# Expert passes of a two-layer decoder: from one expert a pass to four column groups of 32 tokens

## The reference, cut to what matters

```python
logits = tok @ router_w                       # (520, 16)
scores = softmax(logits); sel = scores + router_bias
# best of 4 groups of 4 experts, then the 2 best experts inside it
combine = one_hot(eidx) * gate                # 2 experts a token, 1040 pairs
a = einsum('md,edf->mef', tok, w1)            # w1, w3: 16 x 1024 x 256 in each layer
b = einsum('md,edf->mef', tok, w3)
g = silu(a) * b * combine[..., None]
y = einsum('mef,efd->md', g, w2)              # w2: 16 x 256 x 1024
```

## Time and profile before

| | us |
|---|---|
| three runs | 1240.48, 1243.84, 1242.88 (median 1242.88) |
| profiled execution, its own time | 1236.9 |
| span of that execution in the trace | 1235.1 |
| mean granted TensorE clock | 0.867 |

### The profile page before, as it was taken

One profiled execution on the slowest core, in us unless ns is written; L12 is line 12 of the kernel. 1 busy time (PEld: TensorE's weight loads), 2 busy tenths in 40 slices (PEclk: granted clock), 3 DMA queues, 4 the chain that ended last, 5 costly groups with the idle time before them and its releaser, 6 DMA issues. The chain is left out here.

```text
span 1235.1 us, 10486 instructions
## 1 busy us (share of the span) xinstructions
PE 999.4 (81%) x3428; PEld 586.6 (47%) x3428; DVE 496.4 (40%) x1014; ACT 195.4 (16%) x452; POOL 291.8 (24%) x372
## 2 busy tenths in 40 slices
PE   6999999999999647976299999943965599999800
PEld 5644466667766512416244444423855244444400
DVE  0044443434323488687632111109286611211147
ACT  2101112212301411002011111121111011111121
POOL 0033032302221022334111122113182112111114
PEclk8999999999999955995589999985585699999965
DMA  6323568447440292446189999528660159998241
GB/s 246 127 80 132 185 211 293 167 170 283 178 140 35 65 317 59 136 140 222 50 274 312 326 332 318 200 71 313 196 220 36 34 195 312 322 341 290 108 171 71
DMA packets 123874, 237.04 MB, mean 192 GB/s; under 512 B 13335, under 2 KB 84559, under 8 KB 123174
## 3 DMA queue, kind: packets, MB, share of 16 engines
q1 hardware_dynamic: 111830, 214.46, 50.2%
q0 software_dynamic: 12000, 22.03, 4.9%
HBM read 226.79 MB, written 67.69 MB: 238 GB/s over the span
## 5 line engine op out<-in xcount | busy, mean ns | idle before, releaser
L331 PE MATMUL banks<-expert_w_a,xT 128*128 128x512 f32 x576 | 257.4, 601 | 1.2 <-ACT glu_gate L472 1.2
L331 PEld LDWEIGHTS banks<-expert_w_a,xT 128*128 128x128 f32 x576 | 152.5, 270 | 88.1 <-issue 47.1
L1494 PE MATMUL banks<-expert_w_a,moe_rowsT 128*128 128x512 f32 x288 | 131.6, 611 | 4.2 <-DVE moe_rowsT L1607 4.2
L1494 PE MATMUL banks<-expert_w_b,moe_rowsT 128*128 128x512 f32 x256 | 112.5, 592 | 0.0
L1689 POOL DMA_INDIRECT results<-moe_results,moe_put_column x34 | 34.3, 1008 | 300.6 <-DVE moe_results L1616 283.9
L1610 DVE TENSOR_TENSOR moe_gated<-moe_silu,banks 128x256 f32<-128x256 f32 x34 | 14.3, 421 | 216.2 <-ACT moe_silu L1558 216.2
L516 DVE TENSOR_TENSOR qk_rows<-banks,b_in_chunk 128x512 f32<-128x512 f32 x24 | 16.6, 692 | 191.8 <-PE banks L331 121.0
L1494 PEld LDWEIGHTS banks<-expert_w_a,moe_rowsT 128*128 128x128 f32 x288 | 55.0, 196 | 69.0 <-issue 65.7
L1494 PEld LDWEIGHTS banks<-expert_w_b,moe_rowsT 128*128 128x128 f32 x256 | 47.4, 190 | 53.6 <-issue 53.6
L1505 PE MATMUL banks<-expert_w_a,moe_gatedT 128*128 128x512 f32 x144 | 65.0, 594 | 1.0 <-DVE moe_gatedT L1613 1.0
L598 POOL TENSOR_TENSOR rope_parts<-qk_rows,constants 128x128 f32<-128x128 f32 x24 | 18.9, 789 | 198.4 <-DVE qk_rows L516 198.4
(11 more groups left out here) (280 smaller groups left out, 1392.4 us busy)
## 6 DMA issues: line engine op xcount, KB each, us to landing
expert_w_a<-in_moe_w SPq DMA_DIRECT2D x54, 1024.0 KB, 10.6
expert_w_b<-in_moe_w SPq DMA_DIRECT2D x48, 1024.0 KB, 10.7
expert_w_a<-in_w_in SPq DMA_DIRECT2D x10, 2048.0 KB, 7.9
out_s_attn<-in_cache_attn_w SPq DMA_DIRECT2D x8, 2044.0 KB, 17.9
expert_w_a<-in_cache_attn_w SPq DMA_DIRECT2D x32, 256.0 KB
join_results<-results SPq DMA_DIRECT2D x16, 512.0 KB
q_broadcast<-sample_q SPq DMA_DIRECT2D x8, 512.0 KB
rows<-h SPq DMA_DIRECT2D x8, 512.0 KB
```

The source lines that it names most:

```text
L331: last = pe.matmul(bank(k, u % 2), tile_cols(kk, c // 3, t), W[:, (c + 1) % 2, kk], start=kk == 0, stop=kk == KT - 1)
L1494: last = pe.matmul(bank(k, 2 + b), XT[:, kk], w13(slot)[:, kk], start=kk == 0, stop=kk == KT - 1)
```

## The change

A pass still has 128 slots, but they are four groups of 32. Each group belongs to one expert and uses its own quarter of PE's columns, so one pass holds up to three experts. There are 48 groups, twelve passes. Experts 0 to 3 get three groups each; the other twelve are ranked by their number of tokens, and rank r gets `BY_SIZE[r]` groups. The order in which ranks are served is `IN_TURN`. Which expert has which rank is only known at run time: SP reads its number into a register (`k.order`) and addresses the weights by it. What doesn't fit goes to further passes as before. POOL takes the row numbers straight from the table's column instead of copying the column first. The passes are written out instead of looped.

```diff
+GROUP = 32
+PER_PASS = P // GROUP
+NFIXED = 4
+FIXED = [3] * NFIXED
+BY_SIZE = [5, 4, 4, 3, 3, 3, 3, 3, 2, 2, 2, 2]
+IN_TURN = [0, 11, 1, 10, 2, 9, 3, 8, 4, 5, 6, 7]
+CAP = FIXED + [BY_SIZE[r] for r in IN_TURN]
+START = [sum(CAP[:m]) for m in range(NE)]
+GROUPS = [m for m in range(NE) for _ in range(CAP[m])]
+NB = len(GROUPS) // PER_PASS
+LAST = [(START[m] + CAP[m] - 1) // PER_PASS for m in range(NE)]
+MAX_EXTRA = 10
+NCOL = NB + MAX_EXTRA
...
@@ Router.pe_tables
+            last = pe.matmul(bank(k, 7)[:, 256:257 + NCOL], self.SL[:, n], self.valr[:, n],
...
@@ Router.dve, between the ranks and the slot table
-        for j in range(2):
-            L(tt(self.tmp[:], self.oh[:, j], rk, ALU.mult))
-            L(dve.tensor_reduce(self.rank[:, 0, j], self.tmp[:], AX, ALU.add))
...
+        L(stt(out=self.key[:], in0=counts[:, NFIXED:NE], scalar=16.0, in1=cst(k, "tie"), op0=ALU.mult, op1=ALU.add))
+        L(tt(self.larger[:], across(self.key[:], SIZES), b3(self.key[:], SIZES), ALU.is_gt))
+        L(dve.tensor_reduce(self.place[:], self.larger[:], AX, ALU.add))
+        L(tt(self.by_size[:], b3(self.place[:], SIZES), across(cst(k, "slot")[:, 0:SIZES], SIZES), ALU.is_equal))
...
+        L(dve.tensor_reduce(self.room[:, :, NFIXED:NE].rearrange("p c e -> p e c"), self.pick[:], AX, ALU.add))
...
+        L(tt(over[:, 0], counts, room, ALU.subtract))
...
+        L(tt(self.spots[:], self.oh[:], self.spot[:].unsqueeze(1).to_broadcast([P, 2, NT, NE]), ALU.mult))
+        L(dve.tensor_reduce(self.at[:], self.spots[:].rearrange("p j t e -> p (j t) e"), AX, ALU.add))
+        L(tt(self.ge[:], b3(self.at[:], NCOL + 1), across(cst(k, "edge"), 2 * NT), ALU.is_gt))
...
+        tt(self.SL[:], across(cst(k, "slot"), 2 * NT), b3(self.slot[:], P), ALU.is_equal).then_inc(self.slots, 1)
...
+        L(dve.tensor_reduce(self.key[:], self.turn_of[:], AX, ALU.add))
+        L(dve.tensor_copy(k.order[l][:], self.key[:]))
@@ experts, sync
-        with sp.Fori(1, NE // NW) as q:
-            for c in range(NW):
...
-                sp.wait_ge(y_done, 4 * q + (c - 3))
+        for m in range(NW, NE):
+            r = IN_TURN[m - NFIXED]
+            e = sp.value_load(k.order[l][0:1, r:r + 1], min_val=NFIXED, max_val=NE - 1)
+            rows = [A[n][l, bass.ds(e, 1)].rearrange("o (k p) f -> p (o k) f", p=P)
+                    for n in ("moe_w1", "moe_w3", "moe_w2")]
+            c = m % NW
+            b, s = (k.w13a, k.w13b)[c // 2], c % 2
+            sp.wait_ge(y_done, LAST[m - NW] + 1)
+            sp.dma_start(b[:, s, :, 0:DE], rows[0]).then_inc(w_in[c], 16)
+            sp.dma_start(b[:, s, :, DE:2 * DE], rows[1]).then_inc(w_in[c], 16)
+            sp.dma_start(w2(c), rows[2]).then_inc(w_in[c], 16)
@@ experts, tensor
+        def up_groups(i, b):
+            for kk in range(KT):
+                for q in range(PER_PASS):
+                    g = slice(GROUP * q, GROUP * q + GROUP)
+                    last = pe.matmul(bank(k, 2 + b)[g], XT[:, kk, g], w13(GROUPS[PER_PASS * i + q] % NW)[:, kk],
+                                     start=kk == 0, stop=kk == KT - 1)
+            return last
+        def down_groups(i):
+            for hh in range(2):
+                for f in range(2):
+                    for q in range(PER_PASS):
+                        g = slice(GROUP * q, GROUP * q + GROUP)
+                        last = pe.matmul(bank(k, 5 + hh)[g], GT[:, f, g],
...
-        def step(q, c):
-            i = 4 * q + c
+        def step(i):
             pe.wait_ge(x_kept, 2 * (i + 1))
-            pe.wait_ge(w_in[c % 4], 48 * (q + c // 4 + 1))
+            for m in sorted(set(GROUPS[PER_PASS * i:PER_PASS * (i + 1)])):
+                if START[m] // PER_PASS == i:
+                    pe.wait_ge(w_in[m % NW], 48 * (m // NW + 1))
...
-            up(c % 4, c % 2).then_inc(h_done, 1)
+            up_groups(i, i % 2).then_inc(h_done, 1)
...
-                down((c - 1) % 4).then_inc(y_done, 1)
+                down_groups(i - 1).then_inc(y_done, 1)
...
-        with pe.Fori(0, 3) as q:
-            for c in range(3, 7):
-                step(q, c)
+        for i in range(NB):
+            step(i)
...
@@ experts, gpsimd
-                take_get(bass.ds(i + NW, 1), c, fetches)
-                hold(fetches, i + 1)
-                gather(c, e_got if isinstance(i, int) and i + NW == NE else got[c])
+                gather_pass(i + NW, e_got if i + NW == NB else got[i % NW])
...
-            take_put(bass.ds(i, 1), c, stores)
-            hold(stores, i + 1)
-            hold(y_kept, 2 * i + 2)
-            scatter(c, put[c])
+            pool.wait_ge(y_kept, 2 * i + 2)
+            scatter_pass(i)
```

More of the change, by code:

```diff
@@ L90, in constants @@
     c["eidx"] = np.tile(np.arange(16, dtype=np.float32), (P, 1))
+    place = [NFIXED + IN_TURN.index(r) for r in range(SIZES)]
+    c["room"] = np.tile(np.array([[GROUP * START[m] for m in place], [GROUP * CAP[m] for m in place]], np.float32
+                                 ).reshape(1, -1), (P, 1))
+    c["tie"] = np.tile(np.arange(SIZES - 1, -1, -1).astype(np.float32), (P, 1))
+    c["edge"] = np.tile((P * np.arange(NCOL + 1) - 0.5).astype(np.float32), (P, 1))
+    c["blocks"] = np.tile((P * np.arange(4)).astype(np.float32), (P, 1))
     c["mhalf"] = np.full((P, 1), -0.5, np.float32)
@@ L1181, in dve @@
         m5 = self.m5
-        dve.memset(self.beyond[:, 0], 1.0)
-        dve.memset(self.beyond[:, 5], 0.0)
+        for m in range(NFIXED):
+            dve.memset(self.room[:, 0, m:m + 1], float(GROUP * START[m]))
+            dve.memset(self.room[:, 1, m:m + 1], float(GROUP * CAP[m]))
         L(dve.memset(self.LG[:], 0.0))
@@ L1248, in dve @@
[L1248 to L1259, removed]
+        stt = dve.scalar_tensor_tensor
+        across = lambda x, n: x.unsqueeze(1).to_broadcast([P, n, x.shape[1]])
@@ new lines, in dve @@
+        L(tt(over[:, 0], counts, room, ALU.subtract))
+        L(tt(self.blocks[:], b3(over[:, 0], 4), across(cst(k, "blocks"), NE), ALU.is_gt))
+        L(dve.tensor_reduce(over[:, 1], self.blocks[:], AX, ALU.add))
+        L(dve.tensor_tensor_scan(upto[:], cst(k, "ones")[:, 0:NE], over[:, 1], 0.0, ALU.mult, ALU.add))
+        L(tt(x0[:], upto[:], over[:, 1], ALU.subtract))
+        tt(self.past[:], rk, across(room, NT), ALU.is_ge)
+        L(stt(out=over[:, 2], in0=x0[:], scalar=float(P), in1=room, op0=ALU.mult, op1=ALU.subtract))
@@ new lines, in dve @@
+        tt(self.spot[:], rk, across(start, NT), ALU.add)
+        L(stt(out=over[:, 3], in0=over[:, 2], scalar=float(P * NB), in1=start, op0=ALU.add, op1=ALU.subtract))
+        L(tt(self.past[:], self.past[:], across(over[:, 3], NT), ALU.mult))
+        L(tt(self.spot[:], self.spot[:], self.past[:], ALU.add))
+        L(tt(self.spots[:], self.oh[:], self.spot[:].unsqueeze(1).to_broadcast([P, 2, NT, NE]), ALU.mult))
+        L(dve.tensor_reduce(self.at[:], self.spots[:].rearrange("p j t e -> p (j t) e"), AX, ALU.add))
@@ L1399, in dve @@
         k, l, L, tt = self.k, self.l, ch.link, dve.tensor_tensor
[L1400 to L1420, removed]
+        shape = [P, MAX_EXTRA, NE]
+        number = cst(k, "slot")[:, 0:MAX_EXTRA].unsqueeze(2).to_broadcast(shape)
+        tt(self.lo[:], number, k.extra_first[l][:].unsqueeze(1).to_broadcast(shape), ALU.is_ge)
+        L(tt(self.hi[:], number, k.extra_upto[l][:].unsqueeze(1).to_broadcast(shape), ALU.is_ge))
+        L(tt(self.lo[:], self.lo[:], self.hi[:], ALU.subtract))
+        L(tt(self.lo[:], self.lo[:], cst(k, "eidx").unsqueeze(1).to_broadcast(shape), ALU.mult))
+        dve.tensor_reduce(self.xf[:, 0:MAX_EXTRA], self.lo[:], AX, ALU.add)
+        L(dve.tensor_copy(self.xf[:, MAX_EXTRA:MAX_EXTRA + 1], k.extra_upto[l][:, NE - 1:NE]))
+        L(dve.memset(k.get[l][:, NCOL:NCOL + 1], 8192))
+        return dve.tensor_copy(k.extras[l][:], self.xf[:])
 def experts(k, st, l):
@@ L1529, in _ @@
         turn_x(0).then_inc(x_turned, 1)
-        for c in range(3):
-            step(0, c)
-        with pe.Fori(0, 3) as q:
-            for c in range(3, 7):
-                step(q, c)
[L1535 to L1538, removed]
+        for i in range(NB):
+            step(i)
+        pe.wait_ge(gT_kept, NB)
+        pe.wait_ge(y_kept, 2 * (NB - 1))
+        down_groups(NB - 1).then_inc(y_done, 1)
         def body(j):
@@ L1648, in _ @@
         k.dve_n = ch.n
-        for c in range(3):
-            step(0, c)
-        with dve.Fori(0, 3) as q:
-            for c in range(3, 7):
-                step(q, c)
-        step(0, NE - 1)
-        keep_last_y(0, NE)
-        dve.wait_ge(put[0], 16 * (NE // NW))
+        for i in range(NB):
+            step(i)
+        keep_last_y(NB)
+        dve.wait_ge(put[0], 16 * (NB // NW))
         def body(j):
@@ L1691, in scatter, with gather_pass @@
                                     ).then_inc(signal, 16)
-        for i in range(NW):
-            take_get(slice(i, i + 1), i, columns)
-        pool.wait_ge(columns, NW)
+        def gather_pass(i, signal):
```

(27 more changed lines are left out.)

147 lines of the change are left out of this document (73 added, 74 removed).

## The result

| | before | after |
|---|---|---|
| median of the runs (lowest to highest), us | 1242.31 (1240.48 to 1243.84, 4 runs) | 1348.43 (1343.95 to 1349.91, 4 runs) |
| profiled execution, its own time, us | 1236.9 | 1349.91 |
| mean granted TensorE clock | 0.867 | 0.803 |

The ratio is 1.0849, 95% interval 1.0818 to 1.0880: slower by 106 us on the medians. The forecast was 1350.

What follows compares the result with a forecast made beforehand. PE was taken to set the pace, with weight transfers close behind. Layer 1 +49, layer 0 +51 and routing +8 made +108 on 1236.9, 1345, or 1350 as a median; range 1300 to 1395.

Steps and rivals of the forecast that it cites:

- Part 1: Expert stages: no further pass, 11 steps of 11.8 us and a last `down`; 56 us less per layer.
- rival (b): Grouped `up` and `down`: groups of 32 columns don't run four at once; 1597 or 2090 us; chance 0.06.
- The factor 2.38: Grouped matmuls: measured speedup for three column tiles; by that estimate the 24 steps take 67 us more.
- Part 2: PE's waits for weights in the expert stages: buffers come free later; 90.8 us more a layer.
- the double stall: Step 9 of a layer: PE waits for two experts' loads, 13.3 + 9.5 = 22.8 us.
- Part 3: TensorE clock: PE idles in six long stalls, slowing the `up` after each by 2.4; 14.4 us more a layer.
- Part 4: Routing, between ranks and slot one-hots: 23 DVE operations instead of 13; 4 us more a layer, bounds 3 and 6.
- (a): Expert stages: the weights keep up and the kernel gets faster, 1153 to 1159 us; chance 0.08, 0.10 with its near side.
- (c): Routing: tokens are left over, each further pass costing 15 us a layer; 1365 to 1380 us; chance 0.04.

Runs made afterwards that it cites:

- e3: The changed kernel with w1 and w3 reloaded after the old expert's last `up`, w2 after its last `down`; 1160.20 us, ratio 0.9346.
- e6: The changed kernel with the edit of e3 and another order of ranks (`IN_TURN`) chosen for it; 1144.16 us, ratio 0.9214.

## Why the prediction was right

**The total and the layers.** Predicted were +51 for layer 0, +49 for layer 1 and +8 for routing; measured on the traces +50.7, +49.7 and +7.0, together 107.4. The profiled executions lie 113.0 apart. The 5.6 between stand ahead of routing 0, in code that the change leaves alone (last section). The medians, 106 apart, agree with the sum of the stages. That each layer comes out within 1 us is luck in part: in the sum the clock behind the long stalls is 3.1 and 2.3 us too dear, the steps 2 too cheap (both below).

**Part 1, passes.** No further pass ran: each layer shows 96 transposes of rows, 8 for each of twelve passes. The step is 11.97 instead of the 11.8 predicted; 0.57 over the plain 11.40, where 0.4 stood with bounds 0 and 0.8. Over eleven steps that is 2 us a layer too little. L326's and L1305's rows of 8 columns were the right ones to go by: at 32 columns 64 matmuls take 7.07, as long as 16 plain ones, and rival (b), two groups at a time or one, falls with that. The factor 2.38 of the Trainium skill (TensorE: Matmul & The Clock Gate, Part 3) does not appear in this trace.

**Part 2, buffers.** This was the step that decided, and its table held stall by stall. Predicted for layer 0: steps 4, 6, 7, 8 and 10 13.3 each, step 9 22.8, step 3 1.5, step 1 1.8. Measured there: 12.9, 13.6, 13.8, 13.4 and 12.7; 21.1; 1.6; 3.7. In layer 1 step 3 was 2.8, and the long ones within 0.3 of layer 0's. Sums 92.7 and 90.2 against 92.6 and 90.8. Two sizes were off and cancelled in layer 0: the double stall was 1.7 shorter (number 9, behind number 8, landed 8.5 later, where 9.5 stood for such a load), and the wait for expert 2 was 1.9 longer.

**Part 3, clock.** Predicted 14.4 a layer; the six `up` after the long stalls took 8.5 to 9.8 instead of 7.07, together 11.3 and 12.1 more. Mis-sized by a fifth: I had taken the mean of two first `up` that followed longer stretches in which PE was mostly idle. Step 1 of layer 0, with its stall of 3.7, added 1.7 that I had not counted.

**Part 4, routing.** Predicted +4 each, measured +3.4 and +3.6. DVE's timeline, against the earlier trace rows: the first of these operations, the costliest of them, and the slot one-hots behind the last:

```profile
606.70 0.17 DVE L1273 SCALAR_TENSOR_TENSOR route_size_key<-banks,constants 128x12 f32<-128x12 f32 x1 [0.65 <-PE banks L1190]
...
607.93 0.46 DVE L1277 TENSOR_TENSOR route_room_pick<-route_by_size,constants 128x288 f32<-128x288 f32 x1
...
613.41 1.49 DVE L1301 TENSOR_TENSOR route_slot_one_hot<-constants,route_slot_of_token 128x1280 f16<-128x1280 f32 x1
```

From 606.70 to 613.41 are 6.7 us; 7.2 stood in the working.

**The rivals.** (a), weights that keep up, came out false for this kernel, but its price was right for another: 1153 to 1159 was its time, and e3, which frees w1 and w3 one `up` into the last step, has 1160. Its condition was one and a half steps between release and need; for the experts without a whole step between, e3 gives the rest of that last step, 4.9, and one whole step, 16.9 us or 1.4 steps. That the price fits so well is not shown to be more than chance: e6 came in below it, at 1144, so the 9.5 us a load behind another that (a) was worked out from are not the least. (c), left-over tokens: none.

## What to carry to other kernels

Count, for every rotating buffer, the whole steps between the last use of the old content and the first use of the new: the transfer must fit into these. Packing more experts into one pass shortens the compute but uses up buffers faster, so the prefetch that hid a load before can be gone though no load got longer. Before paying for more buffers, look at what holds the one there is: here w1 and w3 waited for a `down` that reads only w2, and the order of ranks alone was worth 106 us.

## What the runs showed of the hardware beyond that

The clock can make the same code differ by some microseconds ahead of the change. In the attention of both kernels PE waits 2.58 us for ACT, at the same point, and then runs at half clock for a while. The stretch from 400.4 to 414.0, before and then after:

```profile
400.40:414.00 13.60, 10.85 (x70) 8.96 (x71) 6.14 (x36) 8.09 (x36) 0.00 (x0) 0.87 0.02 4
```

```profile
400.40:414.00 13.60, 12.58 (x52) 10.41 (x52) 3.27 (x19) 6.45 (x29) 0.00 (x0) 0.50 0.01 2
```

The granted clock is 0.87 in one and 0.50 in the other, 70 matmuls against 52. From the end of that wait to the third group of score products behind it are 9.3 us before and 12.7 after, so 3.4 of the 5.6 arise here. Why the clock stayed low longer in one of them is not shown. Over the ten profiled executions of this study routing 0 reached the same instruction (L1261 after, L1233 before) between 599.3 and 604.9 us, the kernel before being the earliest and the kernel after the latest; others with the changed routing lie between. So 5 us between two single executions prove nothing here, and the medians and the stages are what to compare.
